# A seven-product scheme for the weight units of the merging stage of a hybrid encoder layer

## What is computed

```python
xn   = rmsnorm(x, norm1_g)
proj = xn @ w_in    # columns: b_a | c_a | x_a | qkv | z | beta | alpha | gate_a | gate_b
u    = causal_conv3(c_a * x_a)
y_a  = (b_a * u) @ w_a_out                        # 512 -> 1024
o    = gated_delta_rule(conv4 + silu of q, k, v; beta, alpha)
y_b  = (rmsnorm(o) * silu(z)) @ w_b_out           # 512 -> 1024
mixed = sigmoid(gate_a) * y_a + sigmoid(gate_b) * y_b
h    = x + mixed @ w_o
y    = rmsnorm(h + relu(rmsnorm(h) @ w_up)**2 @ w_down, final_g)
```

## Time and profile before

| | us |
|---|---|
| median of three runs | 1717.41 |
| span of the profiled execution, first to last instruction | 1717.9 |
| merging stage, unbroken run of TensorE from 434.20 to 882.37 | 448.2 |
| TensorE busy in the span | 1689.5 |
| VectorE busy in the span | 1070.0 |
| GpSimd busy in the span | 362.6 |

### The profile page before, as it was taken

How to read it: one execution, slowest core, us unless ns; L and a number is a source line. 1 busy time by engine, 2 the same in 40 slices (tenths; PEclk the granted TensorE clock), 3 DMA queues, 4 the chain that set the end, 5 groups by cost and what they waited for, 6 DMA issues and landing times.

```text
span 1717.9 us, 25485 instructions
## 1 busy us (share of the span) xinstructions
PE 1689.5 (98%) x10389; PEld 1585.0 (92%) x10389; DVE 1070.0 (62%) x1448; ACT 636.3 (37%) x1125; POOL 362.6 (21%) x409
## 2 busy tenths in 40 slices
PE   6999999999999999999999999999999999999998
PEld 6999999999999999999998889999998889999986
DVE  5566536765511234432262498888888878777786
ACT  5222224544211111111142354555555444444444
POOL 1000023344355565656500110000003000000001
PEclk9999999999999999999999999999999999999999
DMA  6011102001756666666543136655653554555543
GB/s 199 26 37 50 55 39 54 2 4 30 233 191 212 204 208 193 204 193 195 185 141 117 50 123 188 190 187 185 191 188 111 163 169 148 160 159 160 180 151 122
DMA packets 205358, 240.27 MB, mean 140 GB/s; under 512 B 9114, under 2 KB 167527, under 8 KB 205244
## 3 DMA queue, kind: packets, MB, share of 16 engines
q1 hardware_dynamic: 196604, 207.20, 39.5%
q0 software_dynamic: 8640, 31.46, 4.7%
HBM read 197.53 MB, written 41.10 MB: 139 GB/s over the span
## 4 chain that ended last, share of the span: by engine, by line
PE 81%; DVE 4%; issue 1%; ACT 1%; POOLq 0%; POOL 0%; DVEq 0%; ACTq 0%
PE ps L1972 26%; PE ps L2927 19%; PE ps L2956 18%; PE ps L2868 6%; PE ps L2939 2%; PE ps L1390 2%; PE ps L1413 1%; PE ps L319 1%; DVE w_lo L2563 1%; PE ps L1487 0%; PE ps L1329 0%; PE ps L1472 0%; PE ps L1496 0%; PE ps L2880 0%; PE ps L1509 0%
## 5 line engine op out<-in xcount | busy, mean ns | idle before, releaser
L2563 DVE TENSOR_TENSOR w_lo<-ff_raw,w_hi 128x1024 fp32r<-128x1024 f32 x225 | 276.3, 1234 | 70.8 <-ACT w_hi L2327 70.8
L2327 ACT CAST w_hi<-ff_raw 128x1024 fp32r<-128x1024 f32 x225 | 233.6, 1050 | 161.2 <-PE ps L2956 123.9
L1972 PE MATMUL ps<-xn_hi,g_hi 128*128 128x384 f32 x672 | 225.9, 336 | 0.0
L1972 PE MATMUL ps<-xn_hi,g_lo 128*128 128x384 f32 x672 | 224.5, 334 | 0.0
L1972 PE MATMUL ps<-xn_lo,g_hi 128*128 128x384 f32 x672 | 224.5, 334 | 0.0
L2927 PE MATMUL ps<-x_half,w_hi 128*128 128x320 f32 (+1 forms) x832 | 194.0, 303 | 0.5 <-ACT hid L2364 0.5
L1757 DVE TENSOR_TENSOR g_lo<-g_raw,g_hi 128x1024 fp32r<-128x1024 f32 x36 | 48.4, 1345 | 171.8 <-ACT g_hi L1747 171.8
L2927 PE MATMUL ps<-x_half,w_lo 128*128 128x320 f32 (+1 forms) x512 | 154.9, 302 | 0.0
L2927 PEld LDWEIGHTS ps<-x_half,w_hi 128*128 128x128 f32 x832 | 142.2, 189 | 1.7 <-issue 0.9
L2671 DVE TENSOR_TENSOR rows<-ps,rows 128x512 f32<-128x512 f32 x210 | 136.4, 684 | 2.6 <-PE ps L2956 1.8
L1972 PEld LDWEIGHTS ps<-xn_hi,g_hi 128*128 128x128 f32 x672 | 126.1, 188 | 1.0 <-issue 0.9
(11 more groups left out here) (343 smaller groups left out, 3691.0 us busy)
## 6 DMA issues: line engine op xcount, KB each, us to landing
ff_raw<-ff_sums SPq DMA_DIRECT2D x120, 512.0 KB, 3.7
ff_sums<-ff_prep POOLq DMA_DIRECT2D x60, 512.0 KB, 4.1
ff_raw<-in_w_down SPq DMA_DIRECT2D x57, 512.0 KB, 4.3
ff_raw<-in_w_up SPq DMA_DIRECT2D x48, 512.0 KB, 3.7
ff_prep<-in_w_up SPq DMA_DIRECT2D x32, 512.0 KB, 4.6
g_raw<-in_w_in SPq DMA_DIRECT2D x28, 512.0 KB, 6.2
ff_prep<-in_w_down SPq DMA_DIRECT2D x56, 256.0 KB, 3.4
w_raw<-in_w_in SPq DMA_DIRECT2D x16, 512.0 KB, 3.9
```

Of the source, the lines that this page charges most:

```text
L1972: last = nc.tensor.matmul(ps[:, bank_of(n), 0:NW], a[:, u % 3, w], x[:, c, rows_of(g)], start=(c == 0 and m == 0), stop=(c == ks - 1 and m ...
L2327: nc.scalar.copy(hi[slot(t, j)][:, :], raw_of(t, j)).then_inc(hi_done, 1)
L2563: nc.vector.tensor_tensor(lo[s][:, :], raw_of(t, j), hi[s][:, :].bitcast(F32), ALU.subtract).then_inc(lo_done, 1)
```

## The change

The 28 units of `w_in` are taken as 14 pairs (gate b 4, then C, X, B twice, then gate a 4). Pair 0 is computed as before. For the other 13 the first two thirds of the rows are treated as a 2 x 2 block product (two output tiles and two halves of the inner dimension on one side, two halves of the inner dimension and two thirds of rows on the other) with seven products instead of eight; the last third takes four plain products. That makes 11 steps of 12 matmuls, where it was 12.

- **Weight sums.** VectorE forms `S1` to `S4` of each pair in place, and hi and lo halves of 8 forms of 512 columns are made instead of 2 units of 1024.
- **Row sums.** GpSimd makes four sums of the input's quarters in the opening, and stores them to DRAM (`x_sums`); they are loaded and split at the start of the merging stage. The opening's VectorE waits for the stores at tile 10.
- **Joins.** Partial results are copied out of PSUM (`keep`, ScalarE), and joined with others by VectorE (`join`), for three of four quarters.
- **Order.** All pairs come first, then eight output units. Gates after tanh are stored to DRAM (`gates`) by ScalarE's queue, branch A's product too (`branch_a`), and loaded again for the output units.
- **SyncE's queue.** The 60 lots are spread over 32 slots: two per pair from pair 2 on, and one per output unit.
- **Closing.** `mixed` and the places of `w_o` move, and the order of their splits.

The core of the diff:

```diff
+                pool.wait_ge(n_lo, 2 * RT)
+                for half in range(2):
...
+                    summed(sum_a, h12, h11, ALU.subtract)
+                    summed(sum_b, l12, l11, ALU.subtract)
+                    summed(sum_a, sum_a[:, :, :], sum_b[:, :, :], ALU.add)
+                    nc.gpsimd.dma_start(self.x_sums[0, :, top], sum_a[:, :, :]).then_inc(sum_a_out, 16)
...
+                    if tile == 10:
+                        dve.wait_ge(sum_a_out, 64)
+                        dve.wait_ge(sum_b_out, 32)
...
+        FORMS = ("A11", "A12", "A21", "S2", "S1", "S3", "S4", "A22")
+        STEPS = (("A11", (0, 0), "U", True, False), ("A11", (0, 2), "V0", True, False), ("A12", (1, 0), "Z", True, True),
+                 ("A12", (1, 2), "V0", False, True), ("A21", (0, 2), "V1", True, False), ("S2", 1, "U", False, False),
+                 ("S1", 0, "Y", True, False), ("S3", 2, "U", False, False), ("S4", (1, 1), "Y", False, True),
+                 ("A22", 3, "U", False, True), ("A22", (1, 2), "V1", False, True))
...
+        Y_UNITS = [("yb", 0), ("yb", 1), ("ya", 0), ("ya", 1), ("yb", 2), ("ya", 2), ("yb", 3), ("ya", 3)]
...
+        def load(sp, p, m):
+            if p >= 3:
+                sp.wait_ge(lo_done, lot(p - 2, "A22"))
...
+        SLOTS = 2 * (NP - 2) + NY
+
+        def lots(sp, n, part):
+            a, b = [(n + x) * SETS // SLOTS for x in range(2)]
+            for x in ([a] if part == 0 else range(a + 1, b)):
+                prep_load(sp, x)
...
+            load_sum(sp, 2)
+            z_load(2)
+            z_load(3)
+            sp.wait_ge(step_done, 2 * NT - 1)
+            load_sum(sp, 3)
+            for p in range(2, NP):
+                for m in range(2):
+                    lots(sp, 2 * (p - 2) + m, 0)
+                    load(sp, p, m)
+                    lots(sp, 2 * (p - 2) + m, 1)
...
+            y_lots(0)
+            y_lots(1)
+            for s, base in gate_out:
+                sp.wait_ge(s, base + 32 * 2)
+            sp.wait_ge(o_lo, H)
+            load_gates(sp, "gb", 0)
+            load_gates(sp, "gb", 1)
+            sp.wait_ge(step_done, PHASE)
...
+            for s, base in gate_out:
+                sp.wait_ge(s, base + 32 * 4)
+            load_gates(sp, "ga", 0)
+            load_gates(sp, "ga", 1)
+            y_lots(2)
+            sp.wait_ge(dve_evac, dve_count["y", 0, 1, NT - 1])
+            load_gates(sp, "gb", 2)
+            y_lots(3)
...
             (VectorE, pair p)
+                times(p, "V0")
+                rest(dve, p, "A22")
+                if more:
+                    weight_sum(dve, p + 1, "S1")
+                    rest(dve, p + 1, "A11")
+                    rest(dve, p + 1, "A12")
+                    rest(dve, p + 1, "A21")
+                    weight_sum(dve, p + 1, "S3")
...
+                join(p, "C22")
...
             (VectorE, output units)
+                if i + 2 < NY:
+                    rest_y(dve, i + 2)
+                if i == 1:
+                    for f in range(TA):
+                        y_rest("ya", f)
...
             (TensorE, one step)
+                if (name, out) == ("A22", "U"):
+                    pe.wait_ge(dve_evac, dve_count[p, "C22"])
...
             (TensorE, output units)
+                pe.wait_ge(*((o_lo, H) if kind == "yb" else (a_lo, TA)))
```

More of the change, by code:

```diff
@@ new lines, in middle @@
+        N_FIRST = len(ALLOCS)
+        ALLOCS += [("y", i, m, g) for i in range(NY) for m in range(2) for g in range(NT)]
+        nth = {x: n for n, x in enumerate(ALLOCS)}
+        FIRST_ORDER, Y_ORDER = (3, 5, 7, 4, 6, 0, 1, 2), (3, 0, 1, 2, 5, 7, 4, 6)
+        banks = [FIRST_ORDER[n % 8] if n < N_FIRST else Y_ORDER[(n - N_FIRST) % 8] for n in range(len(ALLOCS))]
+        bank = lambda x: banks[nth[x]]
+        before = lambda n: max((m for m in range(n) if banks[m] == banks[n]), default=None)
@@ L1855, in scalar, with sum_split, first_gate @@
-            for u in range(NU):
-                kind = UNITS[u][0]
-                if u + 2 < NU:
-                    split(act, u + 2)
+            tanh = lambda out, x: nc.scalar.activation(out, x, ACT.Tanh, scale=0.5)
+            def sum_split(n):
+                s, base = sums_in[n]
+                act.wait_ge(s, base + 16)
+                nc.scalar.copy(t_hi[n], t_val[n]).then_inc(sum_hi, 1)
+            def first_gate(m, g):
+                if (m, g) == (0, 0):
+                    act.wait_ge(self.rule.stored, 16 * (H + 1))
+                act.wait_ge(step_done, NT * m + g + 1)
+                tanh(gate_tile[0][m][:, rows_of(g)], ps[:, bank((0, m, g)), 0:NW]).then_inc(act_evac, 1)
@@ new lines, in keep, with final @@
+            def keep(p, n):
+                s, name, m, g = ((0, "U", 0, 0), (5, "U", 0, 1), (6, "Y", 1, 1))[n]
+                act.wait_ge(step_done, step(p, s))
+                if n == 0:
+                    place_free(p)
+                if n == 2 and PAIRS[p][0] == "B":
+                    act.wait_ge(conv, 5 * (2 * PAIRS[p][1] + 2))
+                nc.scalar.copy(place(p, m, g), ps[:, bank((p, name)), 0:NW]).then_inc(kept, 1)
+            def final(p, name):
+                if not by_act(p):
+                    return
+                s, m, g = {"V0": (3, 0, 2), "U": (9, 1, 0), "V1": (10, 1, 2)}[name]
+                act.wait_ge(step_done, step(p, s))
+                out, x = place(p, m, g), ps[:, bank((p, name)), 0:NW]
+                (nc.scalar.copy(out, x) if PAIRS[p][0] == "C" else tanh(out, x)).then_inc(act_evac, 1)
@@ new lines, in factor, with join @@
+            def factor(p, m, g):
+                return c_sb[m][:, rows_of(g)] if PAIRS[p][0] == "X" else acc[m][:, rows_of(g)]
+            def join(p, name):
+                s, x, n = {"C11": (2, "Z", 1), "C22": (7, "U", 3), "C12": (8, "Y", 2)}[name]
+                m, g = int(name[1]) - 1, int(name[2]) - 1
+                dve.wait_ge(kept, KEPT + 3 * (p - 1) + n)
+                dve.wait_ge(step_done, step(p, s))
+                tensor(place(p, m, g), ps[:, bank((p, x)), 0:NW], place(p, m, g), ALU.add).then_inc(dve_evac, 1)
+                if not by_act(p):
+                    dve.wait_ge(dve_evac, dve_count[p, name])
+                    tensor(place(p, m, g), factor(p, m, g), place(p, m, g), ALU.mult).then_inc(dve_evac, 1)
@@ L1961, in vector @@
[L1961 to L1974 removed]
+            for f in range(2):
+                dve.wait_ge(z_in[f], 32)
+                tensor(o_gated[f], z_gate[f % 2][:, :], o_gated[f], ALU.mult).then_inc(o_mul, 1)
@@ new lines, in vector, with products @@
+            closing.vector_split(dve, range(4, 6))
+            closing.vector_mix(dve, range(7, 8))
+            closing.vector_split(dve, range(6, 8))
+            closing.vector(dve)
+        def products(w_hi, w_lo, x_hi, x_lo, out, w_of, ks, start, stop, checked=True):
+            for n, c in enumerate(ks):
+                for m, (a, x) in enumerate(((w_hi, x_hi), (w_hi, x_lo), (w_lo, x_hi))):
+                    last = nc.tensor.matmul(out, a[:, w_of(c)], x(c), start=(start and n == 0 and m == 0),
+                                            stop=(stop and n == len(ks) - 1 and m == 2), skip_group_check=not checked)
+            return last
```

1014 lines of the change are left out of this document (672 added, 342 removed).

## The result

The changed kernel took 1781.0 us, the median of four runs (1776.7 to 1783.3), beside 1716.9 us for the kernel before on the same chip: a ratio of 1.037, with an interval of 1.0353 to 1.0386. It is slower by 64 us. The forecast had been slower by 29, with a range that ended at 1768. The profiled span grew from 1717.9 to 1781.5 us, by 63.6.

The account below looks back on a forecast made before the run. TensorE was taken to bound the merging stage, with SyncE's queue of lots only just fast enough. Terms -28.3 + 2 + 41.5 + 13 + 1 = +29.2 us gave a forecast of 1746.6 us, range 1700 to 1768.

Parts of the forecast that it names:

- the lots: In the pairs, lots in SyncE's queue delay the load of the last pair's weights: +41.5 us.
- the opening: GpSimd's 20 row sums beside VectorE slow each other; loss bound by 0 and 4 us, taken as +2.
- the output products: After the pairs, late unit 3 weights are subtracted ahead of branch A's remainders, which unit 2 needs: +13 us (8 to 20).
- the holes at the join: Sign: TensorE idle time ended by VectorE's join `C22`, mostly once per pair in the later pairs.
- the pace of the lots: Sign: lots in SyncE's queue go at 6.7 to 7.2 us each; 6.95 was taken.
- a wait for `ya_lo`: Sign: a wait of some 13 us before the third output unit.
- The matmuls taken away, -28.3: 13 pairs save 12 matmuls each, 27.1 us, and a hole of 1.24 us goes: -28.3 us.
- The clock, +1: Holes of 5 us may lower TensorE's granted clock for a moment, mostly hidden under the queue wait: +1 us.
- The lots are fast enough: Rival: pace under 5.96 us a lot, weights never late, 1 us for the first pair: -12.3, 1705 us; chance 0.17.
- Worse contention: Rival: 7.4 us a lot, 16 us for branch A, 4 opening, 2 clock: +54, 1771 us; chance 0.12.
- The rival that the added traffic costs: Put up with the experiments, no chance given: the scheme's 29.9 MB of added traffic is what costs, as contention.

Follow-up runs that it names:

- experiment 10: The changed kernel with its 60 lots loaded and stored as they are, without GpSimd's four sums: 1737.3 us, 1.0117.
- Experiment 1: The kernel before plus only GpSimd's 20 row sums, their stores and VectorE's wait at tile 10, with no reader: 1733.0 us, 1.0084.
- Experiments 4: The changed kernel with the lots' transfers issued from GpSimd's queue, two at a time, instead of SyncE's: 1770.9 us, 1.0304.
- Experiment 12: The changed kernel with 36 lots ahead of the last pair's weights and 24 ahead of the output units', for 44 and 16: 1794.7 us, 1.0451.
- Experiment 2: The changed kernel with weights of output units 2 and 3 loaded earlier and VectorE's remainders put behind the merges: 1765.8 us, 1.0274.
- experiment 11: The changed kernel with row sums spaced, output units reordered, lots on GpSimd's queue, loads ahead of waits, and lots without sums: 1711.9 us, 0.9963.
- experiment 5: The changed kernel with row sums spaced, output units reordered, lots on GpSimd's queue, and two loads put ahead of waits: 1762.4 us, 1.0258.
- experiment 8: The kernel before with its own lots moved from SyncE's queue to GpSimd's, two at a time: 1723.6 us, 1.0037.

## Why the prediction was wrong, step by step

The sign was right, and so was the mechanism of the largest term, the lots. The time was missed by 34 us (63.6 of span for a sum of 29.2). Two terms were mis-sized by a large factor, and they make up 30 of it: the opening (+2, measured 14.0) and the output products (+13, measured 30.6). Of the signs named ahead, the holes at the join, the pace of the lots and a wait for `ya_lo` came; the merging stage ended at 946.2 us and not near 912.

**The matmuls taken away, -28.3: right.** Without the lots' sums, experiment 10, the pairs take 326.4 us for an arithmetic 319.8. One hole of 4.5 us makes most of the difference.

**The opening, +2: it was 14.0.** The step that failed is "with little in hand, so I bound the loss by 0 and 4 us". The row that it rested on, 3.62 us for two steps beside GpSimd and 2.91 alone, I read as a slow-down of a quarter. But GpSimd's operations beside them had 256 columns and took 1.15 to 1.75 us. The trace of before had the better sign one row on: a copy of two columns took 0.70 us at 687.93 us beside GpSimd and 0.16 alone. In the opening 20 operations of about 2 us stand nearly one behind the other. The share of 68% was also of the wrong stretch, 100 to 200 us. GpSimd's sums ran from 45 to 97 us. From 44 to 100 us VectorE had been busy 32.3 us of 56 (58%) with 47 operations; in the changed kernel it was busy 46.2 us (83%) and had done 31. From 72.5 to 90.1 us, where TensorE's hole lies, it had next to no idle time (0.41 us) and was the bound. Experiment 1 shows the 14 by themselves.

**The lots, +41.5: right.** The pace came out at 6.95 us, as taken. The first lot left at 473.25 us, which less the opening's 14.0 is 459.25, for the 461 forecast. The load of (13,1) left at 772.7 us. TensorE's start had moved by 14, so by the prediction's own count it was wanted at 730.3: late by 42.4. The whole surplus of the pairs was 367.5 - 319.8 = 47.7. Some 6 us of it are in the first pair, for which the sum had no term and one rival had 1. Its hole of 3.61 us ended with ScalarE's copy of a bank out of PSUM (487.65 us, 0.47 long), and that stood behind the fourth row sum, for whose load ScalarE had waited 8.92 us. Its hole of 2.38 us was one of the ordinary kind, ended by the join `C22` at 495.78. Experiments 4 and 10 show the cause from two sides: another queue takes 28.6 us off, lots without sums 41.1. Experiment 12 is a third: eight lots fewer ahead of the last pair's weights take 34.7 off.

**The clock, +1: within the wait, as said, but not small.** Of the 47.7 us only 31.3 are holes, and the rest is matmuls at a granted clock of 0.95 for 1.00. When the holes went the clock came back (0.98 and 0.99 in experiments 4 and 10). I take it for no extra cost, since the lots set the pace; no experiment shows that by itself.

**The output products, +13: it was 30.6.** The step that failed is "VectorE subtracts them *ahead of* branch A's four remainders", which looked at unit 3 alone. One unit earlier the same order puts the remainder of unit 2 ahead of the merges of unit 0. That is a wait of its own (11.97 us), and the 12.31 us that I had counted came behind it. The count also gave the load 5.5 us to land, where the burst made it 14.8; and the four remainders took 1.8 us each beside GpSimd. Experiment 2 took 13.5 of the 30.6 off by order and earlier loads. With all mends and the shorter lots 105.1 are left (experiment 11), 5.2 over the bare matmuls.

**The rivals.** "The lots are fast enough" fell: over all 60 lots the pace was between 7.2 and 8.3 us from store to store in every form of the changed kernel that kept the sums, and 6.95 up to lot 43 in the changed kernel itself. "Worse contention", 1771 us, was nearer the time than my forecast, but for the wrong reason: it put most of the excess on the pace, which was as forecast. The rival that the added traffic costs, put up with the experiments, fell in the pairs (experiments 10 and 11). In the first 35 us of the output products it may have a part, which no experiment sets apart from the order.

**Where the gain went.** The scheme's 28.3 us are real. The kernel of experiment 5 spends 448.0 us from the streams' end to the output projection, and the kernel before 448.0. The scheme takes 28.3 us from the stage that was the cover for 60 round trips of lots, whose chain had 26.9 us in hand. It also gives VectorE more to do beside GpSimd, and the lots go slower than the 6.76 us of before. With the lots' sums gone the same stage takes 433.6.

**What stays open.** Whether lots whose sums another engine makes would bring the ceiling of 1711.9 us into reach; what makes the pairs differ by 9 us among kernels with the same queue; and why the z gates' loads left later in experiment 8. No version that keeps the sums beat the kernel before. The best took 1752.8 us, and without its closing wait of 24 would still be at some 1729.

## What to carry to other kernels

Before shortening a stage, list what uses it as cover. A helper chain that ran at 6.76 us a lot, where 6.87 would do, became the bound at once, in whichever queue it was put, and after the queue was mended it stood at the stage's other end. Price two engines that hold each other up by the operation that the loser must sit out: a copy of 24 columns cost as much extra as an operation on 1176, and twenty long operations in a row turned a busy share of 58% into a bound. Read that share from the stretch in which the new work will run. When a kernel asks for many loads at one moment, add up the megabytes, and put the load that gates a PSUM bank ahead of them.

## What the runs showed of the hardware

- Beside GpSimd's additions of 768 columns each, the groups of VectorE's operations gained 0.8 to 1.6 us on average, whatever their length: 1.444 to 2.577 us for 1176 columns, 0.174 to 1.239 for 24, 0.161 to 0.966 for 3. GpSimd's own operations took 1.95 to 2.30 us there.
- One core moved 384 to 432 GB/s for 18 us on end, at a DMA share of nine tenths or more, and a load of weights issued then took 14.8 us to land, where the median of `g_raw` loads before was 6.3.
- Pairs that moved 255 GB/s (experiment 10) and 287 GB/s (experiment 11, DMA share 0.85) took 326.4 and 328.5 us, for 319.8 by arithmetic; those of the changed kernel moved 224 GB/s and took 367.5.
- The pairs with eleven holes of 0.8 to 5.0 us had a mean granted clock of 0.95, and the output products with two holes of 12 us had 0.90. Pairs with one hole of 4.5 us had 0.99 (experiment 10), and the merging stage before, with one of 1.2 us, 1.00.
